# The first mixer's softmax division: from the probabilities to the outputs of a head pair

## The reference

```python
def chunked_attention(q, k, v, q_gain, k_gain, rel_bias):
    ...
    def one_chunk(c):
        ...
        s = jnp.einsum('bqhd,bkhd->bhqk', qb, kb).astype(jnp.float32) * scale + bias
        valid = (c * CHUNK + kpos - pad) >= 0
        s = jnp.where(valid[None, None], s, NEG_INF)
        p = jax.nn.softmax(s, axis=-1)
        return jnp.einsum('bhqk,bkhd->bqhd', p.astype(vb.dtype), vb)

def hybrid_mixer(h, w_in, q_gain, k_gain, rel_bias, pool_w, pool_scale, w_out):
    proj = h @ w_in
    ...
    a = chunked_attention(q, k, v, q_gain, k_gain, rel_bias)
    p = multiscale_pool(u, pool_w, pool_scale)
    return jnp.concatenate([a, p], axis=-1) @ w_out
```

## Time and profile before

| | us |
|---|---|
| median of 3 runs (724.35, 724.42, 726.02) | 724.42 |
| the profiled execution | 725.3 |
| its span, first to last instruction | 723.5 |
| TensorE busy | 707.4 (98%) |
| VectorE busy | 485.4 (67%) |
| ScalarE busy | 375.2 (52%) |
| GpSimd busy | 62.1 (9%) |

### The profile page before, as it was taken

One profiled execution on the slowest core, in us unless ns is written; L12 is line 12 of the kernel. 1 busy time (PEld: TensorE's weight loads), 2 busy tenths in 40 slices (PEclk: granted clock), 3 DMA queues, 4 the chain that ended last, 5 costly groups with the idle time before them and its releaser, 6 DMA issues.

```text
span 723.5 us, 9745 instructions
## 1 busy us (share of the span) xinstructions
PE 707.4 (98%) x3740; PEld 597.8 (83%) x3740; DVE 485.4 (67%) x741; ACT 375.2 (52%) x507; POOL 62.1 (9%) x34
## 2 busy tenths in 40 slices
PE   8999999999998999999999999999999999999996
PEld 7888888888886678888888888888888988877884
DVE  5797777655477635876777755476772638798756
ACT  6865445544376344845544544476444533675451
POOL 0000000000002220000000000000005443131001
PEclk9999999999999899999999999999999999999998
DMA  8996545554364225555554556435555413543001
GB/s 287 371 354 260 205 176 178 194 210 174 117 248 159 98 91 219 206 202 181 205 194 174 184 213 245 175 125 224 178 193 190 162 59 116 175 154 137 2 1 58
DMA packets 20675, 128.30 MB, mean 177 GB/s; under 512 B 2432, under 2 KB 3328, under 8 KB 6432
## 3 DMA queue, kind: packets, MB, share of 16 engines
q1 hardware_dynamic: 20160, 127.41, 48.9%
q10 hardware_dynamic: 432, 0.29, 0.1%
q0 software_dynamic: 48, 0.13, 0.0%
HBM read 126.77 MB, written 1.05 MB: 177 GB/s over the span
## 4 chain that ended last, share of the span: by engine, by line
PE 95%; DVE 2%; ACT 1%; DMA 1%; issue 0%; SPq 0%; DVEq 0%
PE ps L391 25%; PE ps L371 16%; PE ps L372 15%; PE ps L373 15%; PE ps L395 13%; PE ps L587 1%; DMA work<-in_xt 1%; DVE work L1598 1%; PE ps L382 1%; PE ps L923 1%; PE ps L409 1%; PE ps L749 1%; PE ps L633 1%; PE ps L464 0%; PE ps L903 0%; PE ps L913 0%
## 5 line engine op out<-in xcount | busy, mean ns | idle before, releaser
L391 PE MATMUL ps<-xt,whi 128*128 128x512 f32 x796 | 201.3, 393 | 0.0
L1402 DVE TENSOR_TENSOR wlo<-raw,whi 128x2048 fp32r<-128x2048 f32 x68 | 156.7, 2313 | 40.5 <-ACT whi L997 40.3
L997 ACT ACTIVATE whi<-raw 128x2048 fp32r<-128x2048 f32 x78 | 148.6, 1908 | 49.3 <-PE ps L373 47.4
L391 PEld LDWEIGHTS ps<-xt,whi 128*128 128x128 f32 x796 | 142.8, 189 | 25.1
L371 PE MATMUL ps<-whi,xt 128*128 128x512 f32 (+1 forms) x304 | 122.1, 402 | 0.1
L373 PE MATMUL ps<-whi,xt 128*128 128x512 f32 (+1 forms) x304 | 117.4, 386 | 0.0
L372 PE MATMUL ps<-wlo,xt 128*128 128x512 f32 (+1 forms) x304 | 117.3, 386 | 0.0
L395 PEld LDWEIGHTS ps<-xt,wlo 128*128 128x128 f32 x796 | 109.1, 190 | 8.0
L395 PE MATMUL ps<-xt,wlo 128*128 128x256 f32 x796 | 111.5, 282 | 0.0
L1355 POOL TENSOR_TENSOR wlo<-raw,whi 128x2048 fp32r<-128x2048 f32 (+1 forms) x10 | 45.5, 4547 | 558.8 <-ACT whi L997 558.8
L1041 ACT ACTIVATE work<-ps 128x512 f32<-128x512 f32 x44 | 26.2, 598 | 97.1 <-PE ps L391 96.8
(11 more groups left out here) (221 smaller groups left out, 686.1 us busy)
## 6 DMA issues: line engine op xcount, KB each, us to landing
raw<-in_gu SPq DMA_DIRECT2D x41, 1024.0 KB, 4.8
raw<-in_dn SPq DMA_DIRECT2D x22, 1024.0 KB, 4.7
raw<-in_win SPq DMA_DIRECT2D x8, 1024.0 KB, 4.7
raw<-in_fqk SPq DMA_DIRECT2D x8, 1024.0 KB, 4.8
raw<-in_wout SPq DMA_DIRECT2D x4, 1024.0 KB, 5.1
raw<-in_fg SPq DMA_DIRECT2D x4, 1024.0 KB, 4.8
raw<-in_fv SPq DMA_DIRECT2D x4, 1024.0 KB, 4.7
raw<-in_fo SPq DMA_DIRECT2D x4, 1024.0 KB, 4.7
```

Source lines behind the costliest of these rows:

```text
L391: return pe.matmul(ps[:, bank, :], wh[:, w[i]], x, start=ks[i] == 0, stop=ks[i] == KD - 1)
L997: act.activation(whi[:, c % RING, 0:n], raw[:, c % RING, 0:n], ACT.Copy).then_inc(hi_ready, 1)
L1402: dve.tensor_tensor(wlo[:, c % RING, 0:n], raw[:, c % RING, 0:n], whi[:, c % RING, 0:n].bitcast(F32), ALU.subtract).then_inc(lo_ready, 1)
```

## The change

The probabilities are no longer scaled. For each pair, VectorE takes the reciprocals of the four columns of sums at once; ScalarE spreads them over 64 equal columns a head (`rinv_wide`, in a part of `XN` that is free then); TensorE transposes the two tiles, which gives for each token, along the row, the reciprocal of the head that the partition belongs to; ScalarE copies that row block from PSUM (`rinv_rows`); and VectorE multiplies the pair's outputs in PSUM by it into `attn1` in SBUF. The pairs take PSUM banks 0 and 1 in turn (pair modulo 2): unscaled outputs in its first half, turned reciprocals in its second. High and low parts are then taken from `attn1`. The low part of chunk `C_WOUT + 3` goes from GpSimd to VectorE.

```diff
+        attn1 = view(XN[:, 0, :], 0, 1024, "p (k s) -> p k s", k=4)
+        rinv_rows = view(XN[:, 1, :], 0, 512, "p (b s) -> p b s", b=2)
+        rinv_wide = view(XN[:, 1, :], 512, 512, "p (b t h d) -> p b t h d", b=2, t=NT, h=2)
...
             def turn_probs(i, h, bank):
...
-                pe.wait_ge(exp_done[i] if i else probs_scaled, 2 * h + 2)
+                pe.wait_ge(exp_done[i], 2 * h + 2)
...
             def values1(pair):
                 pe.wait_ge(pt_ready[0], 2 * pair + 2)
+                if pair >= 2:
+                    pe.wait_ge(a_done[0], pair - 1)
...
-                    pe.matmul(ps[rows, pair // 2, col:col + S], v1[:, 0, d], pt1[:, i, 0:S], start=True, stop=False)
+                    pe.matmul(ps[rows, pair % 2, 0:S], v1[:, 0, d], pt1[:, i, 0:S], start=True, stop=False)
...
+            def turn_rinv(pair):
+                pe.wait_ge(rinv_spread, pair + 1)
+                if pair >= 2:
+                    pe.wait_ge(a_done[0], pair - 1)
+                for t in range(NT):
+                    m = pe.transpose(ps[:, pair % 2, S + t * P:S + (t + 1) * P], rinv_wide[:, pair % 2, t, :, :].rearrange("p h d -> p (h d)"), ident)
+                m.then_inc(rinv_turned, 1)
...
                 turn_probs(0, h, 6 + h % 2)
+                if h >= 2 and h % 2 == 0:
+                    turn_rinv(h // 2 - 1)
...
             attention_out(0, 0)
             values1(H1 // 2 - 1)
+            turn_rinv(H1 // 2 - 1)
...
+            def spread_rinv(pair):
+                act.wait_ge(rinv_ready[0], pair + 1)
+                if pair >= 2:
+                    act.wait_ge(rinv_turned, pair - 1)
+                act.activation(rinv_wide[:, pair % 2, :, :, :], rinv[:, 2 * pair:2 * pair + 2, :].rearrange("p h t -> p t h").unsqueeze(3).broadcast_to([P, NT, 2, DH1]),
+                               ACT.Copy).then_inc(rinv_spread, 1)
+            def row_of_rinv(pair):
+                act.wait_ge(rinv_turned, pair + 1)
+                if pair >= 2:
+                    act.wait_ge(a_done[0], pair - 1)
+                act.activation(rinv_rows[:, pair % 2, :], ps[:, pair % 2, S:2 * S], ACT.Copy).then_inc(rinv_row, 1)
             def outputs_hi(half):
-                act.wait_ge(pv_psum[0], 2 * half + 2)
-                act.activation(a1h[:, 2 * half:2 * half + 2, :], ps[:, half, :].rearrange("p (k s) -> p k s", k=2), ACT.Copy).then_inc(at_hi, 1)
+                act.wait_ge(a_done[0], 2 * half + 2)
+                act.activation(a1h[:, 2 * half:2 * half + 2, :], attn1[:, 2 * half:2 * half + 2, :], ACT.Copy).then_inc(at_hi, 1)
...
-            outputs_hi(0)
+                if h % 2 == 0 and h >= 2:
+                    spread_rinv(h // 2 - 1)
+                if h % 2 and h >= 3:
+                    row_of_rinv(h // 2 - 1)
+                if h == 6:
+                    outputs_hi(0)
...
+            spread_rinv(3)
+            row_of_rinv(3)
             hi(C_WIN + 7 + RING)
...
-            for c in [C_WOUT + 1, C_WOUT + 2, C_WOUT + 3] + list(range(C_FO, C_DQ)):
+            for c in [C_WOUT + 1, C_WOUT + 2] + list(range(C_FO, C_DQ)):
...
-            def scaled(h):
-                dve.wait_ge(exp_done[0], 2 * h + 2)
-                dve.reciprocal(rinv[:, h, :], sums[:, h, :]).then_inc(rinv_ready[0], 1)
-                dve.wait_ge(rinv_ready[0], h + 1)
-                for t in range(NT):
-                    p = probs1[:, h % 2, COL[t]:COL[t] + KEYS[t]]
-                    dve.tensor_scalar(p, p, rinv[:, h, t:t + 1], None, ALU.mult).then_inc(probs_scaled, 1)
+            def rinv_of(pair):
+                dve.wait_ge(exp_done[0], 4 * pair + 4)
+                heads = slice(2 * pair, 2 * pair + 2)
+                dve.reciprocal(rinv[:, heads, :], sums[:, heads, :]).then_inc(rinv_ready[0], 1)
+            def divided(pair):
+                dve.wait_ge(pv_psum[0], pair + 1)
+                dve.wait_ge(rinv_row, pair + 1)
+                dve.tensor_tensor(attn1[:, pair, :], ps[:, pair % 2, 0:S], rinv_rows[:, pair % 2, :], ALU.mult).then_inc(a_done[0], 1)
+            def outputs_lo(half):
+                dve.wait_ge(at_hi, half + 1)
+                k = slice(2 * half, 2 * half + 2)
+                dve.tensor_tensor(a1l[:, k, :], attn1[:, k, :], a1h[:, k, :].bitcast(F32), ALU.subtract).then_inc(at_lo, 1)
...
-            for h in range(0, H1, 2):
-                masked(0, h, bias_of(h), 4)
-                if h:
-                    probs_out(0, h - 1, 6 + (h - 1) % 2)
-                masked(0, h + 1, bias_of(h + 1), 4)
-                scaled(h)
-                scaled(h + 1)
-                probs_out(0, h, 6 + h % 2)
-            attn_lo(0, [0], 0, a1h, a1l)
+            for h in range(H1):
+                masked(0, h, lambda t: bias1[:, h, P:2 * P] if t == 0 else bias1[:, h, :], 4)
+                if h >= 1:
+                    probs_out(0, h - 1, 6 + (h - 1) % 2)
+                if h % 2 == 0 and h >= 2:
+                    rinv_of(h // 2 - 1)
+                if h in (4, 6):
+                    divided(h // 2 - 2)
+            outputs_lo(0)
+            rinv_of(3)
...
             probs_out(0, H1 - 1, 6 + (H1 - 1) % 2)
+            divided(2)
+            divided(3)
...
-            attn_lo(1, [1], 2, a1h, a1l)
-            dve.wait_ge(lo_ready, C_WOUT + 4)
+            outputs_lo(1)
+            dve.wait_ge(lo_ready, C_WOUT + 3)
+            lo(C_WOUT + 3)
```

More of the change, by code:

```diff
@@ L249, in build @@
             [sem(f"{n}_{i}") for i in range(3)] for n in ("s_psum", "neg_ready", "exp_done", "pt_psum", "pt_ready", "pv_psum"))
-        rinv_ready, a_done = [sem(f"rinv_ready_{i}") for i in range(3)], [None] + [sem(f"a_done_{i}") for i in (1, 2)]
-        probs_scaled = sem("probs_scaled")
+        rinv_ready, a_done = [sem(f"rinv_ready_{i}") for i in range(3)], [sem(f"a_done_{i}") for i in range(3)]
+        rinv_spread, rinv_turned, rinv_row = sem("rinv_spread"), sem("rinv_turned"), sem("rinv_row")
         at_psum, at_hi, at_lo = sem("at_psum"), sem("at_hi"), sem("at_lo")
@@ L648, in values1 @@
                 pe.wait_ge(pt_ready[0], 2 * pair + 2)
+                if pair >= 2:
+                    pe.wait_ge(a_done[0], pair - 1)
                 heads = [(slice(DH1 * i, DH1 * (i + 1)), i, slice(DH1 * (2 * pair + i), DH1 * (2 * pair + i + 1))) for i in range(2)]
-                col = pair % 2 * S
                 for rows, i, d in heads:
-                    pe.matmul(ps[rows, pair // 2, col:col + S], v1[:, 0, d], pt1[:, i, 0:S], start=True, stop=False)
+                    pe.matmul(ps[rows, pair % 2, 0:S], v1[:, 0, d], pt1[:, i, 0:S], start=True, stop=False)
                 for rows, i, d in heads:
-                    m = pe.matmul(ps[rows, pair // 2, col + P:col + S], v1[:, 1, d], pt1[:, i, S:S + P], start=False, stop=True)
+                    m = pe.matmul(ps[rows, pair % 2, P:S], v1[:, 1, d], pt1[:, i, S:S + P], start=False, stop=True)
                 m.then_inc(pv_psum[0], 1)
+            def turn_rinv(pair):
[5 more added lines that the diff above has]
+                m.then_inc(rinv_turned, 1)
             u_step(0)
@@ L672, in _ @@
                             m.then_inc(d_psum, 1)
-                if h >= 2 and h % 2 == 0:
-                    values1(h // 2 - 1)
                 if h >= 2:
+                    if h % 2 == 0:
+                        values1(h // 2 - 1)
                     pe.wait_ge(pt_ready[0], h - 1)
                 turn_probs(0, h, 6 + h % 2)
+                if h >= 2 and h % 2 == 0:
+                    turn_rinv(h // 2 - 1)
             def attention_out(nb, p):
@@ L1589, in _ @@
             dve.wait_ge(par_landed, 16)
-            def scaled(h):
-                dve.wait_ge(exp_done[0], 2 * h + 2)
-                dve.reciprocal(rinv[:, h, :], sums[:, h, :]).then_inc(rinv_ready[0], 1)
-                dve.wait_ge(rinv_ready[0], h + 1)
-                for t in range(NT):
-                    p = probs1[:, h % 2, COL[t]:COL[t] + KEYS[t]]
-                    dve.tensor_scalar(p, p, rinv[:, h, t:t + 1], None, ALU.mult).then_inc(probs_scaled, 1)
-            def bias_of(h):
-                return lambda t: bias1[:, h, P:2 * P] if t == 0 else bias1[:, h, :]
-            for h in range(0, H1, 2):
-                masked(0, h, bias_of(h), 4)
-                if h:
-                    probs_out(0, h - 1, 6 + (h - 1) % 2)
-                masked(0, h + 1, bias_of(h + 1), 4)
-                scaled(h)
-                scaled(h + 1)
-                probs_out(0, h, 6 + h % 2)
-            attn_lo(0, [0], 0, a1h, a1l)
+            def rinv_of(pair):
[13 more added lines that the diff above has]
+                if h >= 1:
+                    probs_out(0, h - 1, 6 + (h - 1) % 2)
+                if h % 2 == 0 and h >= 2:
[4 more added lines that the diff above has]
+            rinv_of(3)
             dve.wait_ge(d_psum, 1)
```

## The result

The changed kernel takes 719.86 us (median of 4 runs, 719.59 to 720.05), the kernel before 724.44 us (median of 4). The ratio is 0.9929 with a 95% interval of 0.9916 to 0.9941. Its profiled execution took 719.59 us, its span 717.8 us: 5.7 us less than before. By the medians the gain is 4.6 us, by the ratio 5.1 (0.71% of 724.4); the forecast was 5.2.

What follows compares the result with a forecast made beforehand. TensorE, busy 98% of the span, was taken to bound the kernel; 7.72 - 0.84 - 0.4 - 1.2 = 5.3 us gain, taken as 5.2, gave 719.2 us from 724.4. Its own range was 717.4 to 721, extended to 722.2 for rivals.

Steps and rivals of the forecast that it cites:

- (a): TensorE's first stall, before head 0's transposes of probabilities at 235.67, goes: 3.93 us gained.
- (c): TensorE's second stall of the same kind, before the transposes at 250.39, goes: 1.21 us gained.
- (b): The low clock after the first stall goes; the sequence from 235.67 takes 3.04 instead of 5.62 us: 2.58 us gained.
- (d): Eight added TensorE transposes of reciprocals, two for each of four pairs, cost 0.84 us, at most 1.7.
- (e): Pair 2's transposes, ahead of the pooling product, wait for ScalarE's spread reciprocals: net 0.4 us cost.
- (f): At the stage's end, the last pair's chain makes TensorE wait 1.2 us for the second low part; bounds 0 to 2.6.
- (g): The low part of C_WOUT + 3, moved to VectorE, costs nothing, hidden by the output projection; 4.6 us at most uncovered.
- 1: Rival: the clock falls in the stage all the same; the gain loses 2.6 us, giving 721.8 us; chance 0.10.
- 4: Rival, slower: the last pair's chain causes a wait that lowers the clock; at 7 us it gives 727.5; chance 0.04.
- 2: Rival: the wait for GpSimd passes to another VectorE instruction, pair 0's product or a low part; 720.7 to 722; chance 0.07.
- 3: Rival: the chain through ScalarE, TensorE, ScalarE and VectorE stalls every pair; 722.9 us; chance 0.08.

Runs made afterwards that it cites:

- the two kernels with GpSimd idle: Kernel before, scaling kept, low parts of C_WOUT + 1 and + 2 moved to VectorE, early or both at the end: 718.84 us (0.9919) and 717.96 us (0.9901).
- the single tensor_scalar: Changed kernel plus one useless 128x128 SBUF-to-SBUF tensor_scalar on VectorE while GpSimd works: 720.57 us, ratio 0.9939 to the kernel before.
- the earlier high part: Changed kernel with ScalarE's high part of chunk C_WOUT + 3 ahead of the last row block: 718.21 us, ratio 0.9909 to the kernel before.
- the third low part on GpSimd: Changed kernel with the low part of chunk C_WOUT + 3 back on GpSimd: 723.41 us, ratio 0.9981 to the kernel before.

## Why the prediction came out

The forecast's mechanism held at each step, and the stage's gain in the trace (5.7 us) was 0.4 us above the sum of 5.3 and 0.5 above the 5.2 that I took. By the ratio the gain is 5.1, so the time itself came out on the forecast.

- (a), (c): both stalls are gone, as reckoned (3.93 and 1.21). That they came from GpSimd's work, which the trace of before only suggested by its times, is shown by the two kernels with GpSimd idle and by the single tensor_scalar.
- (b): 5.62 against 3.07 us for the same sequence, 2.55 for 2.58.
- (d): the transposes cost 0.22 us for a pair within the heads (237.03 to 237.72, 0.69, against 0.47 for three transposes alone), 0.28 for the last (256.13 to 256.41, where the values' turn-over falls in), about 1.0 in all with pair 2's 0.27, for 0.84.
- (e): from head 6's transposes to the pooling product 1.20 us (248.35 to 249.55) against 0.71 before; less the transposes' 0.27 that is 0.22 for a reckoned 0.4. Reading one value 64 times over costs ScalarE no more than the 0.43 us that I had reckoned for a plain form: `L1128` takes 0.41 us.
- (f): 0.98 us by the starts (260.89 to 261.87) for 1.2, with exactly the order that was named; the earlier high part took it away. The chain from the last values to the second low part took 5.7 us (256.13 to 261.81) for 6.0.
- (g): the moved low part costs nothing, as reckoned: it was done at 264.02 (261.73 + 2.29), long before its use. What I did not see is that this part earns 3.8 us by the ratios and in the stage (45.35 against 41.55), because two SBUF operands would otherwise have made `outputs_lo` wait. I had cited the Trainium skill's rule on this ("SBUF — State Buffer", "Who interferes with whom"), found no row for it and tied it to GpSimd's chunks as the change leaves them, so the sum was right without having asked what the moved part was for.
- Together: 7.69 us gained (3.93, 1.21 and 2.55) less 2.20 paid (1.0, 0.22 and 0.98) is 5.5. The other 0.2 us of the stage's 5.7 lie in starts of matmuls around the two old stalls and the pooling product, which no term covers. (e) and (f) were each taken 0.2 us too high and (d) 0.15 too low, so the sum is near in part because small errors offset each other.
- One reading was off: the scaling is not "over 3.6" of VectorE's 6.92 us in the window 245 to 255 but 2.63, by its instructions in that window, and 1.46 of these were the wait for GpSimd. Nothing hung on it: VectorE is busy for 5.02 us between 238 and 248 after the change, and its new work stalled no head.
- The rivals: 1 and 4 did not happen, though the third low part on GpSimd shows how near 4's mechanism lay (a wait of 3.05 us at that very place, and the low clock after it). 2 did not happen: the product of pair 0 met GpSimd, but with one operand in PSUM, and the second low part of the outputs met no GpSimd work, since the change had moved that to VectorE. 3 was wrong: pairs 0 and 1 had no wait.

## What to carry to other kernels

When an instruction on VectorE takes several times its usual length, look at GpSimd's timeline in the same microseconds before thinking of its data or of the chain: here 3.2 of the 3.75 us of two instructions were GpSimd's. Ask of each VectorE instruction near GpSimd work what its form is and where its operands lie, also of those that a change turns from PSUM to SBUF: here a tensor_scalar within SBUF and products or differences of two SBUF operands stood still, and small reciprocals within SBUF and everything with an operand in PSUM did not. And before rebuilding the arithmetic, try moving GpSimd's work: two moved instructions gave at least as much here as the whole new division.

## What was not expected of the hardware

A product of two SBUF operands stands for GpSimd as long as a tensor_scalar does (3.88 and 3.75 us beside one GpSimd chunk of 4.5), although the pair ran in 0.63 us otherwise (0.55 as tensor_scalar). The clock can fall after a wait is over: in the kernel with the third low part on GpSimd it was 1.00 in the last microsecond of a 3.05 us wait, 0.79 in the next and 0.50 until 268, while TensorE was busy again; with two SBUF operands in the scaling it fell about 1 us after the end of the 4.06 us wait (1.00 until 237, 0.80 in the next microsecond), and in the kernel before still within the 3.93 us wait. By contrast no wait of 1.34 us or less in any of these kernels was followed by a lower clock.
